# GpSimd's order in the attention slots of a hybrid encoder step: recurrence pieces ahead of attention pieces

## What is computed

```python
q_nope = rmsnorm(q[..., :MLA_NOPE], ...)
q_rope = apply_rope(rmsnorm(q[..., MLA_NOPE:], ...), cos, sin)
k_nope = rmsnorm(einsum('bsr,rhd->bshd', ckv_all, w_uk), ...)
o_mla  = rmsnorm(mla_attention(q_nope, q_rope, pos, k_nope, krope_all, ckv_all, k_pos, w_uv), ...)
# both recurrences: S_t = diag(f_t) S_{t-1} + k_t v_t^T,  o_t = S_t^T q_t
o_hg, s_hg_new   = chunk_recurrence(hq, 1.0 - f, hi, log(f), s_hg)
o_gla, s_gla_new = chunk_recurrence(gq * GLA_DK ** -0.5, gk, gv, log_a, s_gla)
mix = concatenate([o_mla, o_hg, o_gla], axis=-1) @ w_o
```

## Time and profile before

| | |
|---|---|
| median of 3 runs | 3473.13 us (3468.93 to 3477.11) |
| profiled execution, time | 3475.6 us |
| profiled execution, span | 3473.8 us, 53683 instructions |
| mean granted TensorE clock | 0.973 |
| PE busy | 3263.9 us (94%) |
| DVE busy | 1482.5 us (43%) |
| ACT busy | 984.2 us (28%) |
| POOL busy | 775.2 us (22%), 1127 instructions |
| mixer of layer 0 | from 362 us; recurrence slots to about 750 us |
| mixer of layer 1 | from 2048 us; recurrence slots to about 2440 us |

### The profile page before, as it was taken

How to read it: one execution, slowest core, us unless ns; L and a number is a source line. 1 busy time by engine, 2 the same in 40 slices (tenths; PEclk the granted TensorE clock), 3 DMA queues, 4 the chain that set the end, 5 groups by cost and what they waited for, 6 DMA issues and landing times. The chain is left out here.

```text
span 3473.8 us, 53683 instructions
## 1 busy us (share of the span) xinstructions
PE 3263.9 (94%) x20686; PEld 2957.3 (85%) x20686; DVE 1482.5 (43%) x2529; ACT 984.2 (28%) x2029; POOL 775.2 (22%) x1127
## 2 busy tenths in 40 slices
PE   5999888988999999999989988899899999999999
PEld 3989556765999999999989975676679999999999
DVE  3511345655354333443363123565554334433443
ACT  3311334434341111111152223444434111111211
POOL 3211656632120000000051145565303000000000
PEclk8999989999999999999999998899999999999999
DMA  6456211103101111111125421111030111111111
GB/s 201 154 184 193 60 38 52 49 27 105 49 25 61 48 36 36 49 60 36 36 76 168 155 80 57 35 59 32 25 129 25 49 36 52 57 36 36 36 36 52
DMA packets 194296, 237.23 MB, mean 68 GB/s; under 512 B 20713, under 2 KB 168382, under 8 KB 194142
## 3 DMA queue, kind: packets, MB, share of 16 engines
q1 hardware_dynamic: 178844, 198.29, 17.8%
q0 software_dynamic: 11072, 31.45, 2.6%
q10 hardware_dynamic: 4226, 5.40, 0.6%
HBM read 195.53 MB, written 39.56 MB: 68 GB/s over the span
## 5 line engine op out<-in xcount | busy, mean ns | idle before, releaser
L1528 PE MATMUL banks<-act_split,w_split 128*128 128x384 f32 (+1 forms) x8352 | 1401.8, 328 | 10.9 <-DVE act_split L2235 7.9
L1528 PEld LDWEIGHTS banks<-act_split,w_split 128*128 128x128 f32 x8352 | 1384.5, 189 | 25.3 <-DVE act_split L2235 13.1
L1528 PE MATMUL banks<-hidden_split,w_split 128*128 128x384 f32 (+1 forms) x3168 | 525.0, 326 | 0.0
L1528 PEld LDWEIGHTS banks<-hidden_split,w_split 128*128 128x128 f32 x3168 | 522.3, 188 | 0.0
L2272 DVE SCALAR_TENSOR_TENSOR x<-banks,mod,x 128x384 f32<-128x384 f32 (+2 forms) x768 | 353.4, 497 | 186.0 <-PE banks L1528 183.6
L2710 DVE TENSOR_TENSOR hidden_f<-banks,silu_a 128x384 f32<-128x384 f32 x132 | 70.7, 536 | 736.5 <-PE banks L1528 736.5
L1528 PEld LDWEIGHTS banks<-w_split,act_split 128*128 128x128 f32 (+1 forms) x2592 | 316.1, 182 | 18.2 <-issue 14.8
L1528 PE MATMUL banks<-w_split,act_split 128*128 128x264 f32 (+1 forms) x2592 | 327.4, 285 | 0.0
L614 POOL TENSOR_TENSOR norm_sum_n<-norm_sum_n,norm_sq 128x384 f32<-128x384 f32 (+1 forms) x42 | 45.4, 1082 | 801.5 <-ACT norm_sq L962 796.3
L1495 ACT ACTIVATE w_split<-w_raw 128x2048 fp32r<-128x2048 f32 x60 | 112.4, 1906 | 381.3 <-PE banks L1528 381.3
L1489 ACT ACTIVATE hidden_split<-hidden_f 128x384 fp32r<-128x384 f32 x132 | 67.0, 508 | 519.6 <-DVE hidden_f L2710 519.6
(11 more groups left out here) (228 smaller groups left out, 3511.1 us busy)
## 6 DMA issues: line engine op xcount, KB each, us to landing
w_raw<-in_w_ffn_in SPq DMA_DIRECT2D x44, 1024.0 KB, 5.1
w_mod_raw<-in_w_mod SPq DMA_DIRECT2D x41, 1024.0 KB, 5.5
w_raw<-in_w_ffn_out SPq DMA_DIRECT2D x22, 1024.0 KB, 4.9
z_token_major<-z_stage POOLq DMA_DIRECT2D x96, 132.0 KB, 2.1
w_raw<-in_w_in SPq DMA_DIRECT2D x10, 1056.0 KB, 6.5
r_qkg<-z_feature_major SPq DMA_DIRECT2D x16, 576.0 KB, 4.1
r_v<-z_token_major SPq DMA_DIRECT2D x16, 512.0 KB, 3.7
w_raw<-in_w_o SPq DMA_DIRECT2D x8, 1024.0 KB, 7.1
```

Source lines behind the costliest of these rows:

```text
L1528: return T.matmul(out, lhsT, rhs, start=start, stop=stop, skip_group_check=True)
```

## The change

In the front and in the head slots that have a recurrence piece, POOL's recurrence piece of a slot is issued ahead of its attention piece. No instruction is added or removed, the other engines' streams stay as they are, and the marks stay behind both.

```diff
                 for i in range(24):
+                    r_slot(i)
                     if i == 1:
                         z_store(0)
                     elif i == 3:
...
                     elif i >= 10 and i % 4 == 2:
                         k_scale(f"p{(i - 10) // 4}", P, ((i - 10) // 4 + 1) % 2)
-                    r_slot(i)
                     if i in MARK_AT:
                         first_marks(MARK_AT.index(i))
...
                     for h in range(HEADS):
+                        if q < 6:
+                            r_slot(24 + 8 * q + h)
                         if h == 0 and more:
                             z_store(q + 1)
...
                             if more:
                                 marks(q + 1)
-                        if q < 6:
-                            r_slot(24 + 8 * q + h)
                 s = st("n2_pool")
```

## The result

The changed kernel took 3492.12 us (median of six runs, 3487.17 to 3495.12), the kernel before beside it 3468.37: a ratio of 1.0056 with a 95% interval of 1.0046 to 1.0066, so 16 to 23 us slower. The forecast was 3467 us, with a range of 3457 to 3481, and 3492 lies outside it. The profiled execution has a span of 3492.2 us against 3473.8.

The account below looks back on a forecast made before the run. TensorE, busy 94% of the span, was taken as the bound, POOL mattering only where PE waits for it. Heads -14.6, front +6.8 and DVE's products +1 gave -6.8 us off the median 3473.1: forecast 3467 us, range 3457 to 3481.

Parts of the forecast that it names:

- 2.5 is exchanged for 2.3: Head tiles: between rotation and query scale, slot 6's recurrence piece (2.3 us) replaces level 5 and gate products (2.5 us).
- Heads, -14.6 us forecast: Head slots of both layers: shorter level 5 and 6 waits, less new query waits, gain 7.3 us a layer.
- The potential of 31 us: Heads: level 5's waits, some 15.5 us a layer, are the most the order can be worth.
- The account by tiles: Head tiles one to six of a layer keep 2.5, 1.2, 1.7, 1.2, 0.7 and 0 us.
- I cost it at nothing: Head slot 0: its rotary piece with two DMA issues runs behind its products, delaying slot 1's by 2.7 us; cost zero.
- Free: Head slot 7: the next tile's mark comes 1.2 us later, behind two state products; cost zero.
- DVE's cover: Third head tile: key squares end at about 583.4, DVE's sum reads them at 583.89, leaving 0.4 us.
- Front, +6.8 us forecast: Front of both layers: tile 8's queries and past blocks 1 and 3 come later, less a 1.3 us gain in layer 1.
- slot 1's gain: Front slot 1, layer 1: PE's level 1 stands 2.02 us for products behind the rotary piece; 1.3 us goes.
- Rival 1: Head tiles: shorter waits spare low-clock time, 1 to 2 us a tile; with 10 us, 3457 us. Chance 0.20.
- Rival 2: Heads: DVE's sum and the rotation slip, heads give 8 us, the front takes it; 3473 us, no change. Chance 0.19.
- Rival 3: Slots 1 to 3: packed POOL pieces starve DVE's products, 2.7 us each; six give 3482 us. Chance 0.15.

Follow-up runs that it names:

- heads_35: Kernel before, with the recurrence piece first only in head slots 3 and 5: -27.9 us (3443.93 us, ratio 0.9922).
- heads_only: Kernel before, with the recurrence piece first in all 48 head slots and no front slot: +0.5 us (3472.34 us, ratio 1.0007).
- heads_scale_first: Kernel before, with the recurrence piece first in all head slots other than 6, no front slot: -15.2 us (3456.68 us, ratio 0.996).
- front_only: Kernel before, with the recurrence piece first in all 24 front slots and no head slot: +26.3 us (3498.14 us, ratio 1.0076).
- front_scales: Kernel before, with the recurrence piece first only in front slots 10, 14, 18 and 22, ahead of past blocks' key scales: +17.0 us (3489.31 us).
- heads_035: Kernel before, with the recurrence piece first only in head slots 0, 3 and 5: -17.2 us (3453.27 us, ratio 0.9945).
- delay_1: Kernel before, order kept, one unread POOL product added ahead of the key scale of past blocks 1 and 3: +11.6 us (3482.4 us).
- delay_2: Kernel before, order kept, two unread POOL products added ahead of the key scale of past blocks 1 and 3: +13.1 us (3483.9 us).
- delay_4: Kernel before, order kept, four unread POOL products added ahead of the key scale of past blocks 1 and 3: +24.3 us (3495.11 us).

## Why the prediction was wrong

**Right:** the place and the pattern. PE's wait on r_qb fell under 15 us (4.0), level 5 waits next to nothing, the hole before the key scale went, the front lost and the queries' wait took the place of level 5's. The step "2.5 is exchanged for 2.3" held in the third tile: from the rotation's start to the query scale's it was 6.6 us before (595.04 to 601.63) and is 6.5 now (603.52 to 610.05). The wait for q_tm was put at some 20 us and is 34.6. That is not so much time lost: PE reached the transposes sooner, after 1.95 us of work where it had been 3.48, and waited the longer for them.

**Heads, -14.6 us forecast, +0.5 measured.** The potential of 31 us was real: heads_35 takes 27.9, and 26.8 of it by the trace in the head slots. The account by tiles held too, on the stretch that it is about. In the third tile, from the moment PE could have started level 5 to the first load of level 6, it was 8.2 us before (600.50 less 3.43, to 605.25) and is 6.5 in the changed kernel (606.25 less 0.61, to 612.12): 1.7 kept, as forecast. Over all twelve head tiles the traces give 86.3 us before and 72.5 in heads_only, 13.8 kept where 14.6 were forecast. By tiles of layer 0 it is 3.7, 0.1, 1.5, 0.8, 0.8 and 0.0 against the forecast's 2.5, 1.2, 1.7, 1.2, 0.7 and 0.

The step that failed is what the prediction set at nothing, "I cost it at nothing" for slot 0's rotary piece and "Free" for what else moves later. heads_scale_first differs from heads_35 by these slots alone (0, 1, 2, 4 and 7) and is 12.7 us slower, with intervals that don't meet; the forecast's terms and these 12.7 us leave -1.9 of the -14.6. By the traces of that pair 7.8 us lie in the head slots and 4.4 in the fronts, whose order is the same, so the order's own share may be the smaller figure. In the trace of heads_only the stretches from level 0 to level 5 of the head tiles take 5.2 us more than before (285.9 against 280.7), so of the 13.8 us some 7 are left in the head slots; the rest of the span took 4.0 more with its order untouched.

The look at DVE's cover was right and was not enough: in heads_only DVE's sum came 0.46 us after the squares in the third tile, 0.4 had been forecast, and it never waited for POOL. Slot 6's piece ahead of the query scale costs 15.7 us; the prediction had it in its sum, as part of an exchange, and never priced the order without it.

**Front, +6.8 us forecast, +26.3 measured,** the larger error. By parts: tile 8 with slot 1's gain 1.1 forecast, 6.2 measured; the past blocks 5.7 forecast, 18.6 measured. In the traces the two fronts of the changed kernel grew by 6.5 and 7.2 us where 3.5 and 3.3 were forecast, and its heads, which should have shrunk by 7 us a layer, grew by 1.0 and 3.4.

Three steps failed. First, the terms of the sum were too small. PE's stall for block 1's keys grew by 1.6 us in layer 0 (forecast 0.6) and by 2.7 in layer 1 (forecast 1.7), that for block 3's by 2.0 in each (forecast 1.7). Before and after, block 1 in layer 0:

```profile
425.97 0.58 PEld L1524 LDWEIGHTS banks<-cst,k_tm 128*96 128x96 f32 x4 [1.39 <-issue]
```

```profile
431.33 0.57 PEld L1524 LDWEIGHTS banks<-cst,k_tm 128*96 128x96 f32 x4 [3.02 <-issue]
```

and in layer 1:

```profile
2114.57 0.57 PEld L1524 LDWEIGHTS banks<-cst,k_tm 128*96 128x96 f32 x4 [1.11 <-issue]
```

```profile
2127.54 0.66 PEld L1524 LDWEIGHTS banks<-cst,k_tm 128*96 128x96 f32 x4 [3.78 <-issue]
```

In layer 1 DVE's sum of block 1's squares waited 0.93 us for POOL, the one place where that sign came. Second, two costs had no term, or a gain that was not kept: tile 8's keys (their stall went from 0.81 to 2.44 us in layer 0), and slot 1's gain of 1.3, which was 1.4 at level 1 and came back at levels 2 and 3 (+2.0 and +0.8 in the changed kernel). Against that, tile 8's queries lost 0.5 in each layer and not 1.2. In the changed kernel block 1 reads:

```profile
425.69 1.04 POOL L807 TENSOR_TENSOR k_sq<-k_tm 128x512 f32<-128x512 f32 x1
427.12 0.59 POOL L707 TENSOR_TENSOR r_kb<-r_qkg,r_e 128x192 f32<-128x192 f32 x1 [0.40 <-ACT r_e L1085]
427.67 0.72 POOL L714 TENSOR_TENSOR r_qb<-r_qx,r_e 128x256 f32<-128x256 f32 x1
428.35 1.01 POOL L741 TENSOR_TENSOR r_k<-r_qkg,r_e 128x384 f32<-128x384 f32 x1
429.29 0.61 POOL L812 COPY k_tm<-z_tile 128x256 f32<-128x256 f32 x1
429.86 1.35 POOL L814 TENSOR_TENSOR k_tm<-k_tm,a_stats 128x512 f32<-128x512 f32 x1
```

On a solid queue all three products of slot 14 delay the scale, and so does the wait for their decays (0.40); the scale itself took 1.35 us where the fastest take 1.04. All the stalls named come to some 12 to 13 us in both layers, where 6.8 were forecast, and the fronts of the changed kernel are 13.7 us longer. Third, each stall was priced at its length and in its place. In front_only the fronts are 16.3 us longer, and 9.0 us more are lost behind them, in head slots whose order is as before, with 11.0 us more of PE's busy time and a mean granted clock of 0.966 where it was 0.973. The prediction had no term for that in the front.

**Rival 1** (the clock) named something that the traces show, with one sign only. It expected PE's shorter waits to win the clock back (PE's busy time fell by 5.6 us in heads_only and by 15.8 in heads_35), while the front's longer ones were priced without it. **Rival 2** (the wait only changes its name) came near the time of heads_only, but not by its own road: the rotation did not slip (it began 2.0 us ahead of the moment PE could have started level 5 before, 2.1 us in the changed kernel), and the heads kept 13.8 us there. **Rival 3** (starved DVE) fell. The median of DVE's half went from 540 to 612 ns, below the 700 that was named, and heads_35, the fastest kernel, has 615:

```profile
L2413 DVE TENSOR_TENSOR r_qb<-r_qx,r_e x126: 397/612/3277, 363.1 to 2452.2; 128x256 f32<-128x256 f32 x126
```

```profile
L2415 DVE TENSOR_TENSOR r_qb<-r_qx,r_e x126: 400/615/3143, 362.9 to 2401.9; 128x256 f32<-128x256 f32 x126
```

DVE's products did get longer, by 72 and 75 ns in the median. That is the direction in which the Trainium skill's rule of the ports that VectorE and GpSimd share points ("SBUF — State Buffer", Who interferes with whom); no run here parts the ports from other causes, and in the fastest kernel it decides nothing. The Trainium skill's rule that TensorE's clock follows recent activity ("TensorE: Matmul & The Clock Gate", Part 1) fits front_scales, where more stalls go with a granted clock of 0.965 to 0.967 in all four executions. It does not tell which stretch will be slow: heads_35 and heads_035 differ by 0.90 and 0.81 where their instructions are the same.

**Open.** How much of the 10.7 us between heads_35 and heads_035 slot 0's order causes is not shown: the head slots hold 2.4 us of it in the one pair of traces. Which of the slots 0, 1, 2, 4 and 7 carries the 12.7 us was not tried beyond slots 0 and 7. Why the two halves of the change sum to some 27 us and the whole to 19 to 24 was not tried either. That the loss beyond the stalls is the clock's is argued from the granted clock and PE's busy time; no run here holds the clock fixed, and which stretch turns slow can't be told ahead from these rows.

## What to carry to other kernels

Don't reorder a queue by kind of work. Reorder it slot by slot: look in each slot at which of the two pieces PE asks for next, and whether the other would run in a hole (slots 3 and 5 here, 28 us) or in front of a piece that is already last (head slot 6, a loss of 16 us, and front slots 10, 14, 18 and 22, a loss of 17). Look at what the moved piece pushes back as well, and don't set it at nothing because one engine's cover is left: that cost up to 12.7 us here. Where TensorE is 94% busy at two clock levels, a new stall can cost more than its length (2.6 times in delay_1, 1.3 times in delay_2 and delay_4, where the interval also allows its bare length). Read PE's busy time next to the waits, and compare first a stretch that the edit doesn't touch: if that differs as much, the pair of executions shows nothing about the edit.

## What was not expected of the hardware

One late product of 1.04 us, four times in an execution of 3470 us, added 4.4 us of wait and 11.6 us of time (7 to 16 by the interval). Four such products at each place added 18.9 and 24.3 (14 to 28).

And two kernels with the same instructions in the same order up to the first head slot ran that part at different granted clocks, 0.95 and 0.92 up to 362 us, then 0.90 and 0.81 up to 460. By the last past block one was 3.8 us ahead of the other: PE loaded block 3's scaled keys at 460.38 us in heads_35 and at 464.20 in heads_035. That is more than most of the terms of this forecast.
